# An encoder layer on one core: attention rounds in another order, probabilities scaled by POOL, first loads in quarters

## The reference

```python
h = rmsnorm(x, norm1) @ w_in                      # 928 columns
c_q, c_kv, k_rope, u = split(h)                   # 256, 128, 32, 512
q = rmsnorm(c_q) @ w_q_b;  kv = rmsnorm(c_kv) @ w_kv_b     # 8 heads
q_rope, k_rope = rope(q_rope), rope(k_rope)
pr = softmax((q_nope . k_nope + q_rope . k_rope) * scale)  # per head, 512 x 512
attn = pr @ v
pool = window_means(u) - u, mixed by pool_w, times pool_scale
x = x + concat(attn, pool) @ w_out
up = conv3(rmsnorm(x, norm2) @ w_up);  x = x + (silu(gate) * val) @ w_down
x = x + (p @ w_ple_proj) * sigmoid(rmsnorm(x, norm3) @ w_ple_gate + b_ple_gate)
y = rmsnorm(x, final_norm)
```

## Time and profile before

| | |
|---|---|
| time, median of 3 runs | 1295.54 us (1293.98 to 1297.46) |
| the profiled execution: its time, its span | 1296.28 us, 1294.5 us |
| PE matmul busy | 1224.9 us, 95% of the span |
| DVE, ACT, POOL busy | 743.9, 459.6, 162.9 us |
| mean granted TensorE clock | 0.978 of full speed |
| chain that ended last | PE 87%, DVE 9%, ACT 1%, DMA 1% |

### The profile page before, as it was taken

The page is one execution under the profiler, slowest core; times in us unless marked ns, Lnnn a source line. Parts: engine busy times, 40 slices in busy tenths (PEclk is TensorE's granted clock), DMA queues, the critical chain, the costliest instruction groups (busy, mean ns, idle before and its releaser), DMA issues.

```text
span 1294.5 us, 15528 instructions
## 1 busy us (share of the span) xinstructions
PE 1224.9 (95%) x5487; PEld 980.9 (76%) x5487; DVE 743.9 (57%) x1099; ACT 459.6 (36%) x736; POOL 162.9 (13%) x139
## 2 busy tenths in 40 slices
PE   5899679889899999999999999999999999999996
PEld 4687555656578888888888888888788888888885
DVE  5549687776447756555545455555533366347665
ACT  4401455655412333233232323223222234225333
POOL 0037400000055400000000000000000011002100
PEclk9999789999899999999999999999999999999999
DMA  5410000010253313222222222222344444443332
GB/s 184 180 50 19 10 11 1 11 33 1 72 178 95 111 49 98 65 76 86 67 79 65 81 65 81 65 81 65 106 146 146 146 147 146 146 130 101 103 122 90
DMA packets 116114, 113.46 MB, mean 88 GB/s; under 512 B 6291, under 2 KB 98794, under 8 KB 115306
## 3 DMA queue, kind: packets, MB, share of 16 engines
q1 hardware_dynamic: 115776, 112.84, 27.6%
q10 hardware_dynamic: 298, 0.11, 0.0%
HBM read 93.01 MB, written 19.92 MB: 87 GB/s over the span
## 4 chain that ended last, share of the span: by engine, by line
PE 87%; DVE 9%; ACT 1%; DMA 1%; issue 1%; DVEq 0%; SPq 0%; ACTq 0%
PE ps L190 27%; PE ps L192 27%; PE ps L191 27%; PE ps L530 2%; PE ps L517 2%; DVE col L1241 1%; DVE SF L1248 1%; DVE WDHL L1234 1%; PE ps L421 1%; DVE GHL L1236 1%; DVE R L1228 1%; DVE SF L1225 1%; DMA SF<-in_x_prompt 1%; DVE R L1224 1%; DMA XT<-xt_scratch 1%
## 5 line engine op out<-in xcount | busy, mean ns | idle before, releaser
L190 PE MATMUL ps<-XH,WH 128*128 128x512 f32 x1096 | 435.0, 397 | 6.7 <-DVE SF L1140 3.7
L192 PE MATMUL ps<-XH,WL 128*128 128x512 f32 x1096 | 429.0, 391 | 0.0
L191 PE MATMUL ps<-XL,WH 128*128 128x512 f32 x1096 | 428.7, 391 | 0.0
L203 DVE TENSOR_TENSOR WL<-WR,WH 128x1024 fp32r<-128x1024 f32 (+2 forms) x137 | 174.0, 1273 | 191.8 <-ACT WH L198 191.7
L198 ACT ACTIVATE WH<-WR 128x1024 fp32r<-128x1024 f32 (+2 forms) x137 | 139.7, 1020 | 323.9 <-PE ps L192 315.6
L190 PEld LDWEIGHTS ps<-XH,WH 128*128 128x128 f32 x1096 | 207.4, 189 | 53.9 <-DVE WL L203 7.7
L191 PEld LDWEIGHTS ps<-XL,WH 128*128 128x128 f32 x1096 | 207.5, 189 | 44.2 <-issue 2.2
L192 PEld LDWEIGHTS ps<-XH,WL 128*128 128x128 f32 x1096 | 207.0, 189 | 43.4
L973 ACT ACTIVATE SF<-SF,col 128x512 f32<-128x512 f32 x88 | 71.7, 816 | 289.0 <-DVE SF L1342 288.9
L1342 DVE TENSOR_TENSOR SF<-ps,R 128x512 f32<-128x512 f32 x88 | 60.5, 688 | 169.1 <-PE ps L192 163.7
L190 PE MATMUL ps<-GHL,WH 128*128 128x512 f32 x352 | 137.1, 389 | 0.8 <-DVE SF L1342 0.8
(11 more groups left out here) (156 smaller groups left out, 1257.0 us busy)
## 6 DMA issues: line engine op xcount, KB each, us to landing
WR<-in_w_up SPq DMA_DIRECT2D x44, 512.0 KB, 3.8
WR<-in_w_down SPq DMA_DIRECT2D x44, 512.0 KB, 3.6
g_scratch<-SF SPq DMA_DIRECT2D x22, 512.0 KB, 2.8
SF<-g_scratch SPq DMA_DIRECT2D x44, 256.0 KB, 3.7
WR<-in_w_out SPq DMA_DIRECT2D x16, 512.0 KB, 3.7
WR<-in_w_ple_gate SPq DMA_DIRECT2D x16, 512.0 KB, 3.6
WR<-in_w_in SPq DMA_DIRECT2D x8, 512.0 KB, 3.8
xt_scratch<-XT SPq DMA_DIRECT2D x2, 2048.0 KB, 12.9
```

The source lines that it names most:

```text
L190: pe.matmul(out, wh, xh, start=first, stop=False)
L191: pe.matmul(out, wh, xl, start=False, stop=False)
L192: return pe.matmul(out, wl, xh, start=False, stop=last)
L203: dve.tensor_tensor(WL[:, slot(n), base:cols, :], WR[:, slot(n), base:cols, :], WH[:, slot(n), base:cols, :].bitcast(F32), ALU.subtract).t ...
```

## The change

1. **Opening.** `norm1` is loaded by itself (`norm1_in`) and turned first; the other gains are turned later, together with the taps of the convolution. x comes in quarters of 256 features over all tokens, and PE waits before each unit only for the quarter in which it lies. SP no longer waits for the gains, and the second request's quarters alternate with the `w_in` tiles. The split of the first weight tile moves behind the eighth unit on ACT and DVE.
2. **Copies of R.** On ACT, the two `copy_r` move behind the split of weight tile 2.
3. **Rounds.** `project` stands at u % 4 = 1; `weigh` is cut in four pieces instead of two; the two `values` stand at u = 15 and at u = 0 of the next pair; DVE makes the key's low part at u % 4 = 3 and the query's at u % 4 = 0; outputs and weight splits move by one tile or so.
4. **Scaling.** DVE makes only the reciprocal; POOL makes the product.

```diff
-            for t in range(TT):
-                sp.dma_start(xtok[0][:, t, :], x[0][t * P:(t + 1) * P, :]).then_inc(x_in[t], 16)
-            sp.wait_ge(gains_in, 16 * 7)
+            def load_x(s, q):
+                cols = slice(q * 2 * P, (q + 1) * 2 * P)
+                sp.dma_start(xtok[s][:, :, cols], x[s].rearrange("(t p) d -> p t d", p=P)[:, :, cols]).then_inc(x_in[s * TT + q], 16)
+            for q in range(4):
+                load_x(0, q)
             for n in range(2):
                 sp.dma_start(WR[:, n, :, :], wtile(w["w_in"][:, cols_in[n]:cols_in[n] + P])).then_inc(win_in[n], 16)
-            for t in range(TT):
-                sp.dma_start(xtok[1][:, t, :], x[1][t * P:(t + 1) * P, :]).then_inc(x_in[TT + t], 16)
+                load_x(1, 2 * n)
+                load_x(1, 2 * n + 1)
...
             def x_unit(u):          # PE
-                if f == 0:
-                    for t in range(TT):
-                        pe.wait_ge(x_in[s * TT + t], 16)
+                pe.wait_ge(x_in[s * TT + f // 2], 16)
...
             def pair(i, last):      # PE
-                    if u % TT == 2:
+                    if u % TT == 1:
...
-                    if i and u in (2, 5):
-                        weigh(i - 1, 1, (0, 1) if u == 2 else (2, 3))
-                    if u in (10, 13):
-                        weigh(i, 0, (0, 1) if u == 10 else (2, 3))
-                    if u in (11, 14) and not last:
-                        values(i + 1, 0 if u == 11 else 1)
+                    if i and u in (2, 3, 4, 6):
+                        weigh(i - 1, 1, [(2, 3, 4, 6).index(u)])
+                    if u in (10, 11, 12, 14):
+                        weigh(i, 0, [(10, 11, 12, 14).index(u)])
+                    if u == 0 and i:
+                        values(i, 1)
+                    if u == 15 and not last:
+                        values(i + 1, 0)
...
             for u in range(KT):     # ACT
                 x_unit(u)
-                if u == 3:
-                    act.wait_ge(win_in[0], 16)
-                    act.wait_ge(rot_done, 2)
-                    split_w_hi(act, 0, None, 0)
+            act.wait_ge(win_in[0], 16)
+            act.wait_ge(rot_done, 2)
+            split_w_hi(act, 0, None, 0)
             squares(0)
...
-                    if u in (12, 15) and not last:      # ACT
-                        values(i + 1, 0 if u == 12 else 1)
+                    if u == 1 and i:
+                        values(i, 1)
+                    if u == 0 and i:
+                        values(i, 0)
...
             def normalise(i, u):    # DVE
                 dve.wait_ge(exp_done, i * 16 + u + 1)
+                if i or u >= 4:
+                    dve.wait_ge(p_norm, i * 16 + u - 3)
                 dve.reciprocal(...).then_inc(rc_ready, 1)
-                dve.wait_ge(rc_ready, i * 16 + u + 1)
-                dve.tensor_scalar(PB[u % 4], PB[u % 4], col[:, RC + u % 4:RC + u % 4 + 1], None,
-                                  ALU.mult).then_inc(p_norm, 1)
...
             def pair(i, last):      # DVE
-                            lows(i, u // TT + 1)
+                            q_low(i, u // TT + 1)
...
+                    if u % TT == 3:
+                        if u // TT < 2:
+                            k_low(i, u // TT + 2)
+                        elif not last:
+                            k_low(i + 1, u // TT - 2)
...
-                    if u == 9:
+                    if u == 7:
                         split_w_lo(dve, T_ATT, i * 2 + (T_ATT + 2), cols=KT if last else 4)
-                    if u == 9:
+                    if u == 8:
                         split_w_lo(dve, T_ATT + 1, i * 2 + (T_ATT + 3), cols=KT if last else 2)
...
+            def normalise(u):       # POOL
+                pool.wait_ge(rc_ready, u + 1)
+                pool.tensor_scalar(PB[u % 4], PB[u % 4], col[:, RC + u % 4:RC + u % 4 + 1], 1.0,
+                                   ALU.mult, ALU.mult).then_inc(p_norm, 1)
+            for u in range(8 * HEADS):
+                normalise(u)
+                if u % 16 == 3 and u // 16 < HEADS // 2 - 1:
+                    pool.wait_ge(wq_in, (u // 16) * 32 + 64)
+                    rot_columns(T_ATT, 4)
```

More of the change, by code:

```diff
@@ L132, in encoder @@
         g_dram = nc.dram_tensor("g_scratch", (P, FT * NSEQ * S), F32, kind="Internal").ap()
-        ident_in, gains_in, taps_in, tabs_in, edge_in, row_in = (sem(n) for n in (
-            "ident_in", "gains_in", "taps_in", "tabs_in", "edge_in", "row_in"))
+        ident_in, norm1_in, gains_in, taps_in, tabs_in, edge_in, row_in = (sem(n) for n in (
+            "ident_in", "norm1_in", "gains_in", "taps_in", "tabs_in", "edge_in", "row_in"))
         x_in = [sem(f"x_in{i}") for i in range(2 * TT)]
@@ L430, in _ @@
             pe.transpose(ps[7][:, 0:88], prow[0:88, 0, :], ident[0:88, 0:88])
-            pe.transpose(ps[7][:, 88:176], prow[0:88, 1, :], ident[0:88, 0:88]).then_inc(par_tr, 1)
+            pe.transpose(ps[7][:, 88:176], prow[0:88, 1, :], ident[0:88, 0:88])
+            pe.wait_ge(gains_in, 16 * 6)
+            rest = NPAR - N2
+            pe.transpose(ps[7][:, 256:256 + rest], prow[0:rest, 2, :], ident[0:rest, 0:rest]).then_inc(par_tr, 1)
             pe.wait_ge(w_lo, 1)
@@ L746, in _ @@
         def _(act):
-            small = [("norm1", 8), ("norm2", 8), ("norm3", 8), ("q_a_norm", 2), ("kv_a_norm", 1), ("pool_scale", 4),
+            act.dma_start(prow[0:KT, 3, :], w["norm1"].rearrange("(k p) -> k p", p=P)).then_inc(norm1_in, 16)
+            small = [("norm2", 8), ("norm3", 8), ("q_a_norm", 2), ("kv_a_norm", 1), ("pool_scale", 4),
                      ("b_ple_gate", 8)]
@@ L805, in _ @@
                 if n == 0:
+                    copy_r(B_X, 4)
+                    copy_r(B_X + 1, 5)
                     for s in range(NSEQ):
@@ L878, in pair @@
                             q_split(i + 1, u // TT - 2)
-                    if u == 6 and i:
+                    if u == 1 and i:
+                        values(i, 1)
+                    if u == 0 and i:
+                        values(i, 0)
+                    if u == 7 and i:
                         output(i - 1, 1)
-                    if u == 14:
+                    if u == 15:
                         output(i, 0)
-                    if u in (12, 15) and not last:
-                        values(i + 1, 0 if u == 12 else 1)
-                    if u == 7:
+                    if u == 6:
                         if last:
@@ L1092, in _ @@
             dve.wait_ge(par_tr, 1)
[L1093 removed]
+            dve.tensor_copy(par[:, N1:N2], ps[7][:, 0:KT]).then_inc(par_copied, 1)
             dve.wait_ge(par_copied, 1)
@@ L1105, in _ @@
                 x_unit(u)
-                if u == 4:
-                    split_w_lo(dve, 0, 0)
+            split_w_lo(dve, 0, 0)
             dve.wait_ge(par_tr, 2)
-            dve.tensor_copy(par[:, 0:N1], ps[7][:, 0:N1]).then_inc(par_copied, 1)
+            dve.tensor_copy(par[:, 0:N1], ps[7][:, 0:N1])
+            dve.tensor_copy(par[:, N2:NPAR], ps[7][:, 256:256 + NPAR - N2]).then_inc(par_copied, 1)
             for u in range(KT, 2 * KT):
@@ L1229, in rotate, with k_low @@
                                   ALU.add).then_inc(q_rot, 1)
-            def lows(i, j):
+            def k_low(i, j):
                 s, h = divmod(j, 2)
@@ L1234, in lows, with q_low @@
                 dve.tensor_tensor(KL[0:NOPE, s, h, :], ps[1][0:NOPE, :], f32(KH[0:NOPE, s, h, :]), ALU.subtract).then_inc(k_lo, 1)
+            def q_low(i, j):
+                s, h = divmod(j, 2)
                 dve.wait_ge(q_hi, i * 4 + j + 1)
@@ L1271, in pair @@
                             rotate(i + 1, u // TT - 2)
-                    if u == 7 and i:
+                    if u % TT == 3:
[3 more added lines that the diff above has]
+                            k_low(i + 1, u // TT - 2)
+                    if u == 8 and i:
                         output(i - 1, 1)
-                    if u == 15:
-                        output(i, 0)
-                    if u == 9:
+                    if u == 0 and i:
+                        output(i - 1, 0)
+                    if u == 7:
                         split_w_lo(dve, T_ATT, i * 2 + (T_ATT + 2), cols=KT if last else 4)
-                    if u == 9:
+                    if u == 8:
                         split_w_lo(dve, T_ATT + 1, i * 2 + (T_ATT + 3), cols=KT if last else 2)
                 if last:
+                    output(i, 0)
                     output(i, 1)
@@ L1290, in _ @@
             rotate(0, 0)
-            lows(0, 0)
+            k_low(0, 0)
+            q_low(0, 0)
             mix_low(0)
@@ L1294, in _ @@
             rotate(0, 1)
+            k_low(0, 1)
             windows(dve, 0, 0, chained)
@@ L1548, in _ @@
                 diff_low(q)
-            for i in range(1, HEADS // 2):
-                pool.wait_ge(wq_in, i * 32 + 32)
-                rot_columns(T_ATT, 4)
+            def normalise(u):
```

(1 more changed line is left out.)

12 lines of the change are left out of this document (5 added, 7 removed).

## The result

The changed kernel takes 1309.91 us (median of 4 runs, 1308.27 to 1310.57), the kernel before 1296.5 us on the same chip (1293.98 to 1297.88): 1.011 of before, 95% interval 1.0097 to 1.0123. It is about 1.1% slower (1.0% by the medians) where I had forecast 1290.6 and a range of 1282 to 1301.

A forecast was written before the change was run, and what follows sets the result against it. In the attention rounds neither PE nor DVE is full, so waits between them set the pace. 1296.28 - 4.5 (first loads) - 5.2 (copies of R) + 4.8 (attention) = 1291.4, or 1290.6 us against the median; range 1282 to 1301.

The forecast's parts named there:

- First loads: Opening: PE waits only for the first quarter of x and starts at 4.8 instead of 9.65 us; -4.5 us.
- copies of R: Opening, ACT: with the split of weight tile 2 ahead of the copies, PE's 3.65 us stall goes; -5.2 us.
- The chain of the new order: Attention rounds: PE waits 1.76 us behind the rotation, 14 times; 166.25 against 168.96 us, -2.7 us at full clock.
- The rival of a long product: Attention: POOL's multiply takes 1.07 us as in its longest row; +6.3 us, 1296.9, up to 1302; chance 0.10.
- The clock: Attention: 5 half-clock stretches follow PE's waits, at 1.49 us each; +7.5 us, bringing attention to +4.8 us.
- 8 to 13 stretches: Rival, attention: half clock in most groups at the wait for POOL and rotation; 11 stretches give 1299.5 us; chance 0.20.

The follow-up runs named there:

- e1: The kernel before with only the change's opening (first loads) and later copies of R; rounds and product as before: 1286.56 us, ratio 0.9932 to before.
- e8: The kernel before with only the two copies of R moved behind the split of weight tile 2: 1290.86 us, ratio 0.9953 to before.
- e2: The changed kernel with the product back on DVE and POOL's taken out: 1297.43 us, ratio 1.0016 to before.
- e11: e2 with two more reciprocals on DVE behind each rotation, their results unread, to lengthen the wait: 1301.53 us, ratio 1.0057 to before.
- e12: e2 with four more reciprocals on DVE behind each rotation, their results unread: 1308.60 us, ratio 1.0125 to before.
- e5: The changed kernel with the weighing's quarters in twos behind the turns of tiles 2, 6, 10 and 14, inside the wait: 1281.33 us, ratio 0.9876 to before.
- e6: e5 with the two values calls also moved into the wait, behind the turns of tiles 10 and 14: 1273.76 us, ratio 0.9828 to before.
- e9: e6 with DVE's rotation ahead of the maximum at tile 2 of 4: 1265.14 us, ratio 0.9771 to before.
- e10: The changed kernel with only DVE's rotation put ahead of the maximum at tile 2 of 4: 1275.05 us, ratio 0.9845 to before.
- e7: e6 with the product back on DVE: 1279.86 us, ratio 0.9863 to before.
- e3: e1 with the product on POOL and the rounds in the old order: 1297.89 us, ratio 1.0013 to before.

## Why the prediction was wrong

**First loads** (-4.5) and **copies of R** (-5.2): right. Together -9.7 was forecast and e1 gave 9.7; e8 gives the copies 3.5 to 6 us of it (interval 3 to 9), which doesn't contradict the split. That the sum came out to a tenth is luck, as e1's own interval is 6 to 12 us. The working holds too: ACT reaches the unit behind its squares at 22.29 us, for 22.0 in the forecast. In the changed kernel 1.3 us of the gain is lost before tile 3, against e1.

**The chain of the new order**: right. The wait behind the rotation was forecast as 1.76 us and is 1.72 to 1.74 in 12 of the 14 groups, for POOL; the first two, in the first pair, where no weighing stands before them, are 2.73 and 2.75, and the 9.95 us of the first group in the sum allow for that. Groups at full clock: 11.94 for 11.75, 12.96 for 12.9. The product on POOL is 0.69 us (48 of 692 ns) for 0.62:

```profile
L1573 POOL TENSOR_SCALAR SF<-SF,col 128x512 f32<-128x512 f32 x48 | 33.1, 692 | 71.0 <-DVE col L1260 71.0
```

From reciprocal to turn it is 1.00 us for 0.94, all of it the product. The rival of a long product (1.07 us) didn't happen in this order.

**The clock** is the step that failed: "I take 5 ... 5 x 1.49 = +7.5". The groups of the changed kernel exceed those of my sum by 24.1 us instead of 7.5. Two long groups make 11.7 of it (2 x 18.75 against 2 x 12.9); the first pair 2.5 (waits of 2.73 us at half clock), the second pair's first three groups 4.8, the others 2.1, and the part behind tile 7 of the last pair 3.0. Both halves of the step were wrong. The number: the clock fell nine times and not five, behind eight of the 14 waits and once more behind a wait of 1.98 us in the last pair. I reasoned from one wait of 1.42 us that was forgiven and took most waits of 1.76 as forgiven too; e2, e11 and e12 show that the time grows between 1.46 and 1.70 us. The price: I took every stretch at 1.49 us, the one size that the trace before showed in a middle group. Behind a wait, when small matmuls followed, the clock stayed low for over 13 us and cost 5.8 us. By my estimate four more stretches at 1.49 are 6.0 us of the 16.6 that are missing, and the two long ones 8.7 more (5.8 for 1.49 each); the rest lies in the other groups, which take up to 0.2 us more each at full clock, and in one stretch of middle length. A rival had the right mechanism and number (8 to 13 stretches, 0.20) but the same price for each stretch, so it ended at 1299.5, 10 us short.

The trace before had a nearer row than the one that I used. In the group of 12.23 us I named the waits of 1.19 and 1.03 us and left out the 0.55 between them (at 279.00). The group from tile 15 of the second pair has only the 0.55 and the 1.03, less in sum than one wait of 1.76, and half clock behind them; so has the third pair's, while the first pair's (at 206.74) stayed at full clock:

```profile
253.12:265.35 12.23, 10.65 (x47) 6.99 (x46) 9.37 (x20) 6.53 (x15) 0.00 (x0) 0.86 0.00 0
```

**The comparison that I left out**: I treated the wait as fixed by the new order and asked only what it cost. The order leaves PE 3.4 us of work beside a chain of 5.16; two quarters of the weighing and the values calls stood outside it. Filling the wait (e5, e6) or shortening its chain by the rotation ahead of the maximum (e9, e10) turns the same change into a gain.

What stays open: why a clean group and a long one follow the same wait of 1.70 us (e12), and with it how many long ones a run has. That it is the small matmuls which keep the clock low is argued, from four long groups that all held them; no run has put other work in their place. The first pair's waits of 2.5 to 2.7 us in e5 to e7, where no weighing exists to fill them, weren't tried with other work.

## What to carry to other kernels

Price a wait of PE twice: its own length, and the matmuls behind it at half clock, which cost up to 5.8 us behind a wait of 1.72 when the work behind it was small. Ask how often a wait was forgiven, and don't carry that over to one that is 0.3 us longer. Before adding an engine to a chain, list which of PE's independent work can stand between the last producer and the waiting turn; here moving weighing and values there was worth 36 us (e6 against the changed kernel), with no work removed. And test a change of several parts part by part: here one group of edits was worth 9.7 us and two others lost 23.

## What the hardware showed that I had not expected

Lengthening a wait that returns 14 times from 1.46 to 1.58 and 1.70 us raised the time by 4.1 and 11.2 us (e2, e11, e12), where the waits themselves add 1.7 and 3.4. Between 1.46 and 1.70 us the same single wait went from never followed by half clock (none of nine groups) to four of nine. In the four longest stretches behind such a wait the clock stayed at its lower level through 10 to more than 13 us in which PE had no wait at all, and all four held 24 matmuls of 128x128 (0.41 us each there); with the wait at 0.88 us or gone, the same 24 ran at full clock (e5, e10). The Trainium skill ("TensorE: Matmul & The Clock Gate", the section on a second failure mode) tells of a kernel in which frequent short pauses between groups of matmuls make the clock swing between its levels; the runs agree, and they add that the length of such a pause matters by tenths of a microsecond. A POOL product of 128x512 took 0.69 us with its factor from a column, 3.3 us at most beside DVE's weight splits (e3).
